# A language model step on one core: the prompt's top-256 search, by maxima or bit by bit

## The reference

```python
def dsa_prompt(q, k, v, iq, ik, iw):
    kk = min(DSA_TOPK, L // 4)                 # 256
    ...
    def one_block(args):                       # 128 query tokens
        t = i * DSA_QBLOCK + jnp.arange(DSA_QBLOCK)
        sc = indexer_scores(iqb, iwb, ik)      # sum over 8 heads of iw * relu(iq . ik)
        sc = jnp.where((key_pos[None, :] <= t[:, None])[None], sc, -jnp.inf)
        _, idx = lax.top_k(sc, kk)
        ...
        return dsa_attend(qb, ks, vs, idx <= t[None, :, None])
```

## Time and profile before

| What | Value |
|---|---|
| median of three runs | 3435.14 us (3434.82 to 3439.13) |
| span of the profiled execution | 3433.9 us, 55751 instructions; the page gives no other time of it |
| PE busy | 3043.0 us, 89% of the span |
| DVE busy | 1813.0 us, 53% |
| ACT busy | 1282.6 us, 37% |
| POOL busy | 749.2 us, 22% |
| bytes moved by DMA | 240.34 MB, mean 70 GB/s |

### The profile page before, as it was taken

The page is one execution under the profiler, slowest core; times in us unless marked ns, Lnnn a source line. Parts: engine busy times, 40 slices in busy tenths (PEclk is TensorE's granted clock), DMA queues, the critical chain, the costliest instruction groups (busy, mean ns, idle before and its releaser), DMA issues. The chain is left out here.

```text
span 3433.9 us, 55751 instructions
## 1 busy us (share of the span) xinstructions
PE 3043.0 (89%) x21427; PEld 2652.0 (77%) x21427; DVE 1813.0 (53%) x3239; ACT 1282.6 (37%) x2691; POOL 749.2 (22%) x816
## 2 busy tenths in 40 slices
PE   7998887764998969999999988959996999999997
PEld 7798776343565549999999978935665999999997
DVE  2177664795899664333345653414456433334566
ACT  2222453423554443333333432114444333333443
POOL 2200011532111014444300013600001444430002
PEclk9999786885999989999999998959998999999999
DMA  4211003523000012222171102121101222217111
GB/s 128 75 38 33 13 25 84 151 78 123 22 32 19 25 53 86 82 76 76 52 260 38 53 37 56 38 92 62 38 19 56 79 76 79 81 59 257 40 55 53
DMA packets 253820, 240.34 MB, mean 70 GB/s; under 512 B 55890, under 2 KB 213988, under 8 KB 253540
## 3 DMA queue, kind: packets, MB, share of 16 engines
q1 hardware_dynamic: 244820, 217.10, 20.5%
q0 software_dynamic: 8752, 19.81, 1.8%
HBM read 182.69 MB, written 55.89 MB: 69 GB/s over the span
## 5 line engine op out<-in xcount | busy, mean ns | idle before, releaser
L2130 PE MATMUL ffn1u_ps<-ffn1u_x_hi,ffn1u_whi 128*128 128x272 f32 x1232 | 357.8, 290 | 19.8 <-DVE ffn1u_wlo L2233 10.8
L2130 PE MATMUL ffn0u_ps<-ffn0u_x_hi,ffn0u_whi 128*128 128x272 f32 x1232 | 357.9, 290 | 19.7 <-DVE ffn0u_wlo L2233 10.7
L2130 PE MATMUL ffn0u_ps<-ffn0u_x_hi,ffn0u_wlo 128*128 128x272 f32 x1232 | 355.7, 289 | 0.0
L2130 PE MATMUL ffn1u_ps<-ffn1u_x_hi,ffn1u_wlo 128*128 128x272 f32 x1232 | 355.7, 289 | 0.0
L198 PE MATMUL ine_ps<-ine_w_hi,ine_x_hi 128*128 128x256 f32 (+2 forms) x864 | 265.3, 307 | 5.6 <-DVE ine_w_lo L214 5.1
L2130 PEld LDWEIGHTS ffn1u_ps<-ffn1u_x_hi,ffn1u_whi 128*128 128x128 f32 x1232 | 233.6, 190 | 22.0 <-DVE ffn1u_wlo L2233 20.6
L2130 PEld LDWEIGHTS ffn0u_ps<-ffn0u_x_hi,ffn0u_whi 128*128 128x128 f32 x1232 | 233.6, 190 | 21.9 <-DVE ffn0u_wlo L2233 20.5
L198 PE MATMUL ine_ps<-ine_w_hi,ine_x_lo 128*128 128x256 f32 (+2 forms) x864 | 250.5, 290 | 0.0
L198 PE MATMUL ine_ps<-ine_w_lo,ine_x_hi 128*128 128x256 f32 (+2 forms) x864 | 249.9, 289 | 0.0
L2130 PEld LDWEIGHTS ffn1u_ps<-ffn1u_x_hi,ffn1u_wlo 128*128 128x128 f32 x1232 | 233.7, 190 | 0.0
L2130 PEld LDWEIGHTS ffn0u_ps<-ffn0u_x_hi,ffn0u_wlo 128*128 128x128 f32 x1232 | 233.7, 190 | 0.0
(11 more groups left out here) (520 smaller groups left out, 8412.2 us busy)
## 6 DMA issues: line engine op xcount, KB each, us to landing
aT<-scratch_a SPq DMA_DIRECT2D x42, 544.0 KB, 7.6
ffn0u_raw<-in_ffn_w_gu_dram SPq DMA_DIRECT2D x44, 512.0 KB, 4.9
ffn1u_raw<-in_ffn_w_gu_dram SPq DMA_DIRECT2D x44, 512.0 KB, 4.9
scratch_a<-ffn0u_u SPq DMA_DIRECT2D x44, 272.0 KB, 2.2
scratch_a<-ffn1u_u SPq DMA_DIRECT2D x44, 272.0 KB, 2.1
ffn0d_w<-in_ffn_w_down_dram SPq DMA_DIRECT2D x88, 128.0 KB, 2.5
ffn1d_w<-in_ffn_w_down_dram SPq DMA_DIRECT2D x88, 128.0 KB, 2.4
ine_w<-in_w_in_even_dram SPq DMA_DIRECT2D x5, 1024.0 KB
```

Source lines behind the costliest of these rows:

```text
L2130: last = nc.tensor.matmul(ps[:, bank + h, 0:TOK2], wp, xp, start=(begins and k == 0 and n == 0), stop=(k == KH - 1 and n == 2), skip_group ...
```

## The change

The search for the 256 largest becomes a search for the 256th largest value. It starts from `cand` = 0 and settles the 32 bits of the threshold from the sign bit down. For each bit one pass over the row counts the scores that are at least `cand` (`accum_out`), a one-column instruction compares the count with 256, and another flips bits of `cand`. After 32 counting passes `cand` is the 256th largest. `search_end` then marks the scores below it and those equal to it, numbers the equal ones by a running count along the row, and keeps as not chosen those equal ones whose number is too high.

The mask is now 1 for a key that is not chosen and 0 for a chosen one, and the -1e30 stands in `identb`. In `dsa_sample` a counting pass of block 7 and one of block 6 stand together, followed by one compare and one flip for both blocks, so the search begins when the scores of both are there. `EARLY` is 9 of 34 steps, and 7 steps follow each of the first three maxima. In `dsa_out` there are two score buffers instead of one; GpSimd's first copy into one waits for the mask of the block two before, no longer for the begin of the search ahead. `search_plan` counts 33 steps for a block, the last at four times the cost.

```diff
+SIGN_BIT = 31
+def search_round(nc, link, b, scores, junk, cand, cnt, flip):
+    for g, x in enumerate(scores):
+        ins = nc.vector.tensor_scalar(junk[g], x, cand[:, g:g + 1].bitcast(F32), None, ALU.is_ge, ALU.add, accum_out=cnt[:, g:g + 1])
+    link(ins)
+    link(nc.vector.tensor_scalar(flip[:, :], cnt[:, :], float(TOPK), -1.0 if b == SIGN_BIT else float(1 << b), ALU.is_lt, ALU.mult))
+    link(nc.vector.scalar_tensor_tensor(out=cand[:, :], in0=flip[:, :], scalar=(1 << b) >> 1, in1=cand[:, :],
+                                        op0=ALU.bitwise_xor, op1=ALU.bitwise_xor))
+def search_end(nc, link, x, n, cand, below, equal, count, ones, num):
+    thr = cand.bitcast(F32)
+    nc.vector.tensor_scalar(equal, x, thr, None, ALU.is_equal)
+    link(nc.vector.tensor_scalar(below, x, thr, None, ALU.is_lt, ALU.add, accum_out=num))
+    link(nc.vector.tensor_tensor_scan(count, ones.to_broadcast([P, n]), equal, 0.0, ALU.mult, ALU.add))
+    link(nc.vector.scalar_tensor_tensor(out=num, in0=num, scalar=float(TOPK - n), in1=count[:, n - 1:n], op0=ALU.add, op1=ALU.add))
+    link(nc.vector.scalar_tensor_tensor(out=equal, in0=count, scalar=num, in1=equal, op0=ALU.is_gt, op1=ALU.mult))
...
     def search_plan():
-        todo = [(s, k) for s in range(S0, NT) for k in range(TOPK // 8)]
-        cost = [BLOCK[s] + 1.5 for s, k in todo]
+        todo = [(s, k) for s in range(S0, NT) for k in range(SIGN_BIT + 2)]
+        cost = [(BLOCK[s] + 5) * (1 if k <= SIGN_BIT else 4) for s, k in todo]
...
-                        if d > 0 and c == 0:
-                            pool.wait_ge(search_begun, BLOCK.index(t) - S0)
+                        if q >= 2 and c == 0:
+                            pool.wait_ge(b_done, 2 + q - 1)
...
-                link(nc.vector.tensor_copy(identb[:, :], st.ident[:, :]))
+                link(nc.vector.tensor_scalar(identb[:, :], st.ident[:, :], NEG, None, ALU.mult))
+                link(nc.vector.memset(ones[:, :], 1.0))
...
-                    nc.vector.tensor_copy(bias[:, t, t * P:(t + 1) * P], causal[:, :]).then_inc(b_done, 1)
+                    nc.vector.tensor_scalar(bias[:, t, t * P:(t + 1) * P], causal[:, :], -1.0, None, ALU.is_lt).then_inc(b_done, 1)
...
-                    link(nc.vector.max(m8[:, :], src[:, 0:L]))
-                    link(nc.vector.match_replace(wk[:, 0:L], m8[:, :], src[:, 0:L], TAKEN))
...
+                    if k <= SIGN_BIT:
+                        search_round(nc, link, SIGN_BIT - k, [x], [below], cand, cnt, flip)
+                        return
+                    search_end(nc, link, x, L, cand[:, 0:1], below, equal, count[:, 0:L], ones[:, 0:1], num[:, 0:1])
+                    nc.vector.tensor_tensor(bias[:, s % RING_B, 0:L], below, equal, ALU.add).then_inc(b_done, 1)
...
-    EARLY = 10
+    EARLY = 9
...
+                    if k == 0:
+                        dve.wait_ge(dot_added, ONE)
+                        dve.wait_ge(summed, 2)
+                        for a in range(AHEAD):
+                            last = score_rows[a][:, length[a] - P:length[a]]
+                            link(nc.vector.tensor_tensor(last, last, causal[:, :], ALU.add))
+                    if k <= SIGN_BIT:
+                        search_round(nc, link, SIGN_BIT - k, score_rows, [marks[:, a, 0:length[a]] for a in range(AHEAD)], cand, cnt, flip)
+                        return
```

More of the change, by code:

```diff
@@ L1539, in reciprocal_deviation, with search_step @@
                     nc.vector.reciprocal(rstd[0:r, j, :], rstd[0:r, j, :]).then_inc(gained, 1)
-                def top_round(s, k):
+                def search_step(s, k):
                     t = BLOCK[s]
                     L = (t + 1) * P
+                    x = sc[:, (s - S0) % 2, 0:L]
+                    below, equal = marks[:, 0, 0:L], marks[:, 1, 0:L]
                     if k == 0:
+                        link(nc.vector.memset(cand[:, :], 0))
                         dve.wait_ge(dots_added, dot_no[("dots", t, 7, chunks(t) - 1)] + 1)
-                        link(nc.vector.tensor_tensor(sc[:, L - P:L], sc[:, L - P:L], causal[:, :], ALU.add))
-                    src = sc if k == 0 else wk
-                    link(nc.vector.max(m8[:, :], src[:, 0:L]))
-                    link(nc.vector.match_replace(wk[:, 0:L], m8[:, :], src[:, 0:L], TAKEN))
[L1550 to L1553, removed]
+                        link(nc.vector.tensor_tensor(x[:, L - P:L], x[:, L - P:L], causal[:, :], ALU.add))
+                    if k <= SIGN_BIT:
[3 more added lines that the diff above has]
+                    nc.vector.tensor_tensor(bias[:, s % RING_B, 0:L], below, equal, ALU.add).then_inc(b_done, 1)
                 def row_max(i, n):
@@ L1915, in add_dot, with search_step @@
                                                        op0=ALU.mult, op1=ALU.add).then_inc(dot_added, 1)
-                def search_round(a, k):
-                    L = (BLOCK[2 + a] + 1) * P
+                length = [(BLOCK[2 + a] + 1) * P for a in range(AHEAD)]
+                score_rows = [sc[:, a, 0:length[a]] for a in range(AHEAD)]
+                def search_step(k):
                     if k == 0:
[L1920 to L1929, removed]
+                        dve.wait_ge(dot_added, ONE)
[6 more added lines that the diff above has]
+                        return
+                    a = k - SIGN_BIT - 1
+                    n = length[a]
+                    below, equal = marks[:, 0, 0:n], marks[:, 1, 0:n]
+                    search_end(nc, link, score_rows[a], n, cand[:, a:a + 1], below, equal, count[:, 0:n], ones[:, 0:1], num[:, 0:1])
+                    link(nc.vector.tensor_tensor(bias_ahead[:, a, 0:n], below, equal, ALU.add))
@@ L1931, in _ @@
                 for d in range(ONE):
                     add_dot(d)
[L1933 to L1936, removed]
+                link(nc.vector.memset(cand[:, :], 0))
+                link(nc.vector.memset(ones[:, :], 1.0))
+                steps = list(range(SIGN_BIT + 1 + AHEAD))
+                per = -(-(len(steps) - EARLY) // NP_)
@@ L1937, in _ @@
+                for k in steps[:EARLY]:
+                    search_step(k)
                 for p in range(NP_):
@@ L1942, in _ @@
                     nc.vector.tensor_scalar(nm[:, :], mx[:, :], -AS, None, ALU.mult).then_inc(m_done, 1)
-                    for a, k in rounds[EARLY + per * p:EARLY + per * (p + 1)]:
-                        search_round(a, k)
+                    for k in steps[EARLY + per * p:EARLY + per * (p + 1)]:
+                        search_step(k)
                     dve.wait_ge(e_done, p + 1)
```

21 lines of the change are left out of this document (13 added, 8 removed).

## The result

The changed kernel takes **3387.55 us** (median of 4 runs, 3386.24 to 3390.86) against 3434.98 us (3434.32 to 3439.13) for the kernel before, run beside it: a ratio of 0.9862, interval 0.985 to 0.9873. The forecast was 3400 us, 3385 to 3416. The direction holds, and so does the mechanism in the sample stage. Both gains were taken too small, the one in the prompt stage by nearly half, and there half of what came has a cause that the forecast had only in its upper bound.

A forecast was written before the change was run, and what follows sets the result against it. VectorE was taken to bound the sample stage, and in the prompt stage to be a term beside a nearly full TensorE. 3433.9 - 23 (sample) - 12 (prompt) = 3399, with 1.2 around the span 3400 us; range 3385 to 3416.

The forecast's parts named there:

- Rival A: Counting pass at two columns a cycle, 750 ns at 1032 columns; total 3387 us; chance 8%.
- The pass: Counting pass on VectorE: one column a cycle, 1.29 us at 1024 columns and 1.15 at 896.
- Rival B: Counting pass at two cycles a column, as in the scan; slower, total 3498 us; chance 4%.
- R = 3.03: Sample stage: one new round for both blocks takes 3.03 us, against 4.89 for the pair of old rounds.
- End of a search: New closing work on VectorE in the sample stage: 6.7 us at 1024 columns, 6.0 at 896, together 12.7.
- Sample stage: Sample attention: first exponential later, at 680.3 us, then 28.4 a pair; last VectorE work ends at 785.9; gain 23 us.
- Prompt stage: Prompt attention: VectorE loses some 28 us of work, of which 12 us show as gain.
- two thirds of the 18.4: Prompt stage: of the 18.4 us that TensorE's transposes wait for the exponential, 12 us go.
- upper bound of 22: Prompt stage: the gain could pass 22 us, since the window's granted clock of 0.93 can rise too.
- Rival D: Prompt stage: all waits for VectorE go and the clock rises with them; total 3390 us; chance 15%.
- C: Only the sample stage gains; lumps and TensorE's balance eat the rest; total 3412 us; chance 17%.
- four equality compares: Prompt stage: four equality compares in the search ends may be held beside GpSimd's work, 1 us each.

The follow-up runs named there:

- compare_no_count: The changed kernel with each counting pass as a plain comparison without the sum, threshold bits from a constant, so the mask is another one: 3370.17 us, ratio 0.9812.
- prompt_only: The changed kernel with the search by counting in the prompt stage only, the sample stage keeping the old MAX8 and MATCH_REPLACE8 search: 3413.52 us, ratio 0.9936.
- xor_pointer: The changed kernel with each round's xor as a tensor_scalar taking the candidate's column as a scalar, one tensor input in place of two: 3390.14 us, ratio 0.9868.

## Why the prediction was right, and where it was off

- **The number**: 3387.55 us is inside the range, near its lower end. It is also Rival A's 3387 almost exactly, and that is chance: A's reason, two columns a cycle, is refuted below, and where the pass does go so (`compare_no_count`) the time is 3370.17.
- **What bounds it**: right in both stages. VectorE set the pace of the sample stage and no longer does between the maxima, only ahead of the first and at the end; in the prompt stage its load is the steep term.
- **The pass**: "I take that one", one column a cycle, 1.29 and 1.15 us; measured 1.28 and 1.14. The row of 750 ns, Rival A's case, is the rate without the sum, as `compare_no_count` shows. Rival B's 2.3 is the scan's alone (2.29 measured).
- **R = 3.03**: it is 2.79. The step that failed is adding up: 0.1 for each read and full durations for the passes. In the trace a read starts before its pass ends, and the second pass with it, so a round is 0.24 shorter.
- **End of a search**: 12.7 forecast, 769.61 to 782.0 measured, 12.4. The bf16 add, bounded by 0.4 and 1.2 and taken as 0.7, took 0.69.
- **Sample stage**: gain 23 (23.5 by its own 785.9), measured 26.0. First exponential forecast at 680.3, came at 678.75; 28.4 a pair, measured 28.1, 28.7 and 28.6; end at 785.9, came at 783.4. Eleven rounds on the path at 0.24 are 2.6, so R's error is nearly the stage's; the smaller ones (a start 0.5 us later, ends 0.3 shorter) cancel. The page loads did not bind, but only just: TensorE waited 3.9 us for the last pair's at 736.90, where it waits 4.1 for ScalarE's copies a pair earlier. The prediction had them landing 1.3 us after they were wanted (735.91 and 734.6) and gave no reason why that costs nothing; these copies are one.
- **Prompt stage**: gain 12, measured 22. VectorE's loss of 28 came as 31.2. The failed step is "two thirds of the 18.4", the waits behind the exponential: I had only idle time in it. Idle time did fall by 11.0 us (9.2 of them behind the exponential), so the 12 are right for what they count. The other 11.3 are TensorE's own matmuls, with a granted clock of 0.98 in place of 0.93 where the searches run; I had put that into the upper bound of 22, and into Rival D at 15%. Of the rivals D is nearest, and not for its whole reason: half the waits are still there (9.2 of 18.4). C, that only the sample stage gains, is refuted by `prompt_only`.
- **GpSimd**: I looked for held instructions at four equality compares, 1 us each, and called the counting pass not exposed. The pass is not held: 14 of the 128 ran beside a long GpSimd instruction and took no longer than the others. The four equality compares were not held either, but none of them met GpSimd, so that is the schedule and says nothing of the form. Held were 12 one-column xors and one final add of 2.39 us. `xor_pointer` takes the first away without a measurable gain.
- **Left open**: the stretch behind the prompt stage reads 2188.5 us in the one trace of before and 2191.7 in that of the changed kernel, 2190.6 to 2195.0 in those of the experiments; no run was made for it. Whether the second score buffer is needed was not tried: with one buffer the next scores would wait for a search that stands behind work that waits for them. Why the granted clock rises as VectorE gets lighter is shown only as a pairing with shorter waits, in the six traces of the table above.

## What to carry to other kernels

When a change takes load off an engine beside a nearly full TensorE, read how long the same matmuls take at either load, and not only the waits between them: here half the prompt stage's gain was in the matmuls. A row for "nearly the same" instruction can be a factor of 1.7 off: a sum kept on the side takes a compare of 1024 columns from 757 to 1278 ns. Before moving a late first step forward, look which transfer is next in line; here 12 of 14 us were hidden by page loads.

## What the runs showed of the hardware

- GpSimd has two effects on VectorE. A one-column operation with two tensor inputs lasted 2.35 us beside an addition of 2.35 us (0.16 alone); with the second input as a per-partition operand, 0.21 us always. And a one-input compare is held as well when it runs at the double rate, while the same with a sum is not. In `compare_no_count`, VectorE and then GpSimd:

```profile
873.60 2.48 DVE L110 TENSOR_SCALAR dsa_marks<-dsa_sc,dsa_cand 128x768 bf16<-128x768 f32 x1
```
```profile
873.32 2.34 POOL L1519 TENSOR_TENSOR dsa_X<-dsa_X,dsa_gb 64x1024 f32<-64x1024 f32 x1 [0.36 <-ACT dsa_X L1454]
```

  It took 0.62 us at the median, 2.48 here; all 32 passes with the sum at this width took 1.01 at most, six of them beside a long GpSimd instruction.
- A bf16 add of two tensors goes at the double rate too: in the prompt stage 559, 492 and 424 ns at 768, 640 and 512 columns, 67 or 68 ns for 128; at 1024 columns 0.69 us.
- The step between passes of a loading loop grows by some 0.7 us with each page whose number it reads: 3.6 us for 4, 6.3 for 8.
